# Router on the unnormalised rows, output projection by column halves, softmax per block, expert choice per sequence

## The chip, the cores and the metric

The kernel runs on one core of a Trainium2 chip. The metric is the device time of one execution in microseconds; lower is better. A core has five engines that run side by side, each with its own queue: TensorE (PE) for matrix products, VectorE (DVE), ScalarE (ACT), GpSimd (POOL) and SyncE (SP), which here only issues transfers. They wait for one another on semaphores. SBUF is the on-chip memory with 128 partitions; PSUM takes TensorE's results.

## The reference

One hybrid encoder layer on two sequences of 512 tokens of 1024 channels, in float32. What matters here is its end:

```
mixed = concat(attn_out, lru_out)                  # (512, 1024) per sequence
x2    = x + mixed @ w_out
h2    = x2 * rsqrt(mean(x2^2) + eps) * norm2_g
aff   = softmax(h2 @ router_w)                     # 16 experts
gate_vals, tok_idx = top_k(aff.T, 64)              # each expert takes 64 of 512 tokens
xs    = h2[tok_idx]
ys    = (silu(xs @ w_gate[e]) * (xs @ w_up[e])) @ w_down[e] * gate_vals
y     = x2 + scatter_add(ys, tok_idx)
```

The choice is made per sequence; both sequences' 64 tokens form one tile of 128 rows for each expert.

## The kernel before

All products are split: an operand is written as a high part (fp32r) and the remainder, and `product` (L869) issues three matmuls, hi x hi, hi x lo, lo x hi. The 1024 tokens of both sequences are NB = 8 blocks of 128 rows; blocks 0 to 3 (BPS = 4) are sequence 0, blocks 4 to 7 are sequence 1. Before the part that changes come the input projection, the recurrent part and the attention.

**Output projection.** For each block b (L997) TensorE runs `project_out(b, k)` over KC = 8 slices k, each with six matmuls of 512 columns, three for each half of the 1024 columns, into two PSUM banks. For block 0 the slices 0 to 5 are done inside the attention's last slots. In the same loop, one block later, come eight transposes of h2 (L933, for block b-1), and two blocks later the router's products (L1013, 8 slices, 16 matmul instructions, for block b-2). The last rounds of the loop have no projection left. SP loads the residual x_again (one buffer) once x2 of the block before is done (L456), stores x2 into y and h2 into the DRAM tensor h2_rows.

**VectorE** adds x_again for the whole block (L1305), waits for ScalarE's sum of squares (L777) and root (L779), computes the reciprocal and a Newton step (L1311, L1109 to L1112), and writes h2 = x2 * rstd * gain (L1315). ScalarE also copies the transposed h2 out of PSUM (L786).

**Softmax and expert choice.** After the logits of all eight blocks VectorE takes the maximum, ScalarE the exponential (L789), VectorE the sum, the reciprocal and the product (L1321 to L1329). TensorE transposes the affinities, so that experts lie on partitions: 0 to 15 for sequence 0 and 32 to 47 for sequence 1, 512 columns each (L1025). Then CAP // 8 = 8 rounds over 48 partitions (L1336): max gives the eight largest, max_index their positions, match_replace strikes them out. The lists are stacked and transposed (L1343 to L1349); `routed` tells GpSimd that the indices are there.

**Into the experts.** When the output projection is over, SP issues five weight loads (1 MB each) of expert 0, then the last stores, then, once these have landed, one more for up and two for down (L480, L482), then the gate weights of expert 1 (L490; the last two of them after both first gathers have landed). GpSimd computes the low parts of the first six gate rows (L574), copies an index column, and gathers 128 rows of h2 (L586). TensorE transposes them, ScalarE and VectorE write xsT_hi and xsT_lo (L807, L1360), and the first product waits for both halves of xsT_lo. From there on the expert loop runs, 24 rows of weights an expert, each row six matmuls.

Nothing is planned by a tool: every engine's order is that of the written code, and the waits in it are on counts.

Of the kernel before, what the change touches and what calls it, by code (L numbers as in the profile page):

```python
# [38 lines left out]
def layer_program(nc, x0, x1, norm1_g, w_in, q_norm_g, k_norm_g, conv_w, conv_b, lru_w_r, lru_b_r,  # L39
# [44 lines left out]
    vec_rows = at("vec_rows", 1536, [44, P], F32)  # L84
    vecs = at("vecs", 2048, [P, 44], F32)
# [7 lines left out]
    V_CONVW, V_CONVB, V_BR, V_BI, V_LAM = 0, 16, 20, 28, 36  # L93
# [64 lines left out]
    h2T = at("h2T", QUIET, [P, 2, KC, P], F32)  # L158
# [4 lines left out]
    aff_pad = at("aff_pad", R5 + 512, [P, BPS, 48], F32)  # L163
    aff_stat = at("aff_stat", R5 + 512 + 768, [P, 3, NB], F32)
# [11 lines left out]
    aff_work = at("aff_work", R1, [48, 2, S], F32)  # L176
    top_val = at("top_val", R1 + 4 * K, [48, CAP], F32)
    top_idx = at("top_idx", R1 + 4 * K + 256, [48, CAP], U32)
    stacked = at("stacked", R1 + 4 * K + 512, [E, 2, P], F32)
# [21 lines left out]
    assert RAW0 >= R1 + 128 * K  # L201
# [43 lines left out]
    h2T_done, h2T_out, logits_done = sem("h2T_done"), sem("h2T_out"), sem("logits_done")  # L245
    aff_shifted, aff_exp_done, aff_done, affT_done = sem("aff_shifted"), sem("aff_exp_done"), sem("aff_done"), sem("affT_done")
    stacked_done, stackedT_done, routed = sem("stacked_done"), sem("stackedT_done"), sem("routed")
    pad_zeroed = sem("pad_zeroed")
# [136 lines left out]

    block = ctx.enter_context(nc.Block())

    @block.sync
    def _(sp):
        rows = [(0, conv_w[0].rearrange("t (c p) -> (t c) p", p=P)), (16, conv_b[0].rearrange("(c p) -> c p", p=P)),  # L390
                (20, lru_b_r[0].rearrange("d (c p) -> (d c) p", p=P)), (28, lru_b_i[0].rearrange("d (c p) -> (d c) p", p=P)),
                (36, lru_lambda[0].rearrange("d (c p) -> (d c) p", p=P))]
# [60 lines left out]
        for b in range(NB):  # L453
            if b:
                sp.wait_ge(x2_done, b)
# [9 lines left out]
        sp.wait_ge(outproj_done, NB)  # L465
# [4 lines left out]
        sp.wait_ge(x2_done, NB)  # L470
# [8 lines left out]
        sp.wait_ge(h2T_done, 2 * NB)  # L479
# [25 lines left out]
    def _(pool):  # L505
# [62 lines left out]
        pool.wait_ge(scores_done, UNITS)  # L568
        pool.memset(aff_pad[:, :, :], 0.0).then_inc(pad_zeroed, 1)

        pool.wait_ge(outproj_done, NB)
# [3 lines left out]
        pool.wait_ge(routed, 2)  # L575
# [3 lines left out]
        for e in range(4):  # L579
            p = e % 2  # L580
            if e >= 2:
                pool.wait_ge(xsT_done, 2 * (e - 1))
            pool.tensor_copy(idx_now[:, p:p + 1], idx_all[:, e:e + 1]).then_inc(idx_copied, 1)
            pool.wait_ge(idx_copied, e + 1)
            pool.sem_inc(gather_ready, 1)
            pool.indirect_dma_start(xs[:, p, :], None, h2_rows, bass.IndirectOffsetOnAxis(ap=idx_now[:, p:p + 1], axis=0)).then_inc(xs_loaded[p], 16)  # L586
# [12 lines left out]
        with pool.Fori(0, (E - 4) // 2) as pair:  # L599
            e = pair * 2  # L600
            for parity in range(2):
                pool.wait_ge(xsT_done, e * 2 + (2 * parity + 6))
                pool.tensor_copy(idx_now[:, parity:parity + 1], idx_all[:, bass.ds(e + (parity + 4), 1)]).then_inc(idx_copied, 1)  # L603
                pool.wait_ge(idx_copied, e * 2 + (5 + 2 * parity))
# [3 lines left out]
                scatter_step(e + parity, e * 2 + (6 + 2 * parity))  # L608
        for e in range(E - 4, E):
            scatter_step(e, 4 + 2 * (E - 4) + e - (E - 4) + 1)  # L610

    @block.scalar
    def _(act):
# [155 lines left out]
        for b in range(NB + 1):  # L769
            if b < NB:  # L770
                act.wait_ge(x2_done, b + 1)
                if b:
                    act.wait_ge(h2_done, b)
                if b >= 2:
                    act.wait_ge(h2_stored[b % 2], 16 * (b // 2))
                    act.wait_ge(h2T_done, 2 * (b - 1))
                act.activation(h2[:, b % 2, :], x2[:, b % 2, :], ACT.Square, accum_out=sumsq1[:, b:b + 1]).then_inc(sumsq2_done, 1)  # L777
                act.wait_ge(sumsq2_done, b + 1)
                act.activation(root1[:, b:b + 1], sumsq1[:, b:b + 1], ACT.Sqrt, scale=1.0 / D, bias=eps).then_inc(root2_done, 1)  # L779
            if b:  # L780
                c = b - 1
                for h in range(2):
                    act.wait_ge(h2T_done, 2 * c + h + 1)
                    if c >= 2:
                        act.wait_ge(logits_done, c - 1)
                    act.activation(h2T[:, c % 2, 4 * h:4 * h + 4, :], bank[:, 4 + h, :].rearrange("p (k t) -> p k t", k=4),  # L786
                                   ACT.Copy).then_inc(h2T_out, 1)
        act.wait_ge(aff_shifted, 1)
        act.activation(aff_e[:, :, :], aff_e[:, :, :], ACT.Exp).then_inc(aff_exp_done, 1)  # L789
# [43 lines left out]
        act.wait_ge(outproj_done, NB)  # L833
        for j in range(SPLIT):
            hi_row(0, 0, raw_gate, gate_loaded, 16, j)
        turn_hi(xsT_hi[:, 0, :, :], xsT_done, 0, xsT_hi_done)
# [31 lines left out]
    def _(pe):  # L868
# [7 lines left out]
        for step in steps:  # L876
# [13 lines left out]
            elif kind == "vectors":  # L890
                pe.wait_ge(vec_loaded, 5 * 16)
                pe.transpose(bank[:, 0, 0:44], vec_rows[:, :], ident[0:44, 0:44]).then_inc(vec_t, 1)
# [43 lines left out]
        def project_out(b, k):  # L936
# [9 lines left out]
            for h in range(2):  # L946
# [50 lines left out]
        for b in range(NB + 2):  # L997
            if b < NB:
                if b >= 2:
                    pe.wait_ge(x2_done, b - 1)  # L1000
                if b == 1:
                    pe.wait_ge(probT_lo_done, UNITS)
                    pe.wait_ge(mixA_lo_done, HEADS // 2)
                for k in range(0 if b else WO_EARLY, KC):
                    ins = project_out(b, k)
                ins.then_inc(outproj_done, 1)
            c = b - 2
            if 0 <= c < NB:
                pe.wait_ge(h2T_out, 2 * (c + 1))
                if c == 0:  # L1010
                    pe.wait_ge(consts3_loaded, 2 * 16)
                for k in range(KC):
                    ins = pe.matmul(bank[:, 7, c * E:(c + 1) * E], h2T[:, c % 2, k, :], router[:, k, :], start=(k == 0), stop=(k == KC - 1))  # L1013
                ins.then_inc(logits_done, 1)
            c = b - 1
            if 0 <= c < NB:
                pe.wait_ge(h2_done, c + 1)
                for h in range(2):
                    if c:
                        pe.wait_ge(h2T_out, 2 * (c - 1) + h + 1)  # L1020
                    transposes(4 + h, [h2[:, c % 2, (4 * h + i) * P:(4 * h + i + 1) * P] for i in range(4)], h2T_done)

        pe.wait_ge(aff_done, 1)
        for b in range(BPS):
            ins = pe.transpose(bank[0:48, 6, b * P:(b + 1) * P], aff_pad[:, b, :], ident[:, :])  # L1025
        ins.then_inc(affT_done, 1)
        pe.wait_ge(stacked_done, 1)
        for i in range(2):
            ins = pe.transpose(bank[:, 5, i * E:(i + 1) * E], stacked[:, i, :], ident[0:E, 0:E])
        ins.then_inc(stackedT_done, 1)  # L1030


        def rows(first, m, first_bank, l_hi, l_lo, between, inc_last=1):

            for j in range(8):
                if j in between:
                    between[j]()
                pe.wait_ge(row_lo, first + (8 * m + j + 1))
# [21 lines left out]
        pe.wait_ge(xsT_lo_done, 2)  # L1060
# [379 lines left out]
```

## Time and profile before

| | us |
|---|---|
| median of three runs | 1089.27 (1089.07 to 1091.78) |
| span of the profiled execution, first to last instruction | 1093.4 |
| output projection, from block 0's last slices | 377.3 to 470.7 |
| from there to the first expert product | 470.7 to 516.1 |
| experts | 516.1 to 1093.4 |

The profiled execution's own time is given as its span; a clocked time without the profiler is not on record for it, and the span is 4.1 us above the median of the timed runs. Over the whole span PE is busy 91%, DVE 75%, ACT 65%, POOL 31%. "Busy" is time in instructions; an engine that waits for a semaphore is idle. In a timeline row the bracket holds the idle time ahead of the instruction and what ended it; "x8" merges eight instructions that follow one another.

### The profile page before, as it was taken

How to read it: one execution, taken by the hardware profiler on the slowest of the kernel's cores; microseconds unless marked ns; L12 is line 12 of the kernel's file. 1: busy time of each engine (PE TensorE's matmuls, PEld its weight loads, DVE VectorE, ACT ScalarE, POOL GpSimd, SP SyncE). 2: the span in 40 equal slices, each digit the busy share in tenths (PEclk: the TensorE clock that was granted, in tenths of full speed). 3: DMA queues.
4: the chain of work that ended last, by engine and by line, in shares of the span. 5: the costliest groups of instructions: out<-in, count | busy, mean ns of one | idle time of the engine just before them, and what ended most of it. 6: DMA issues, size and time to landing. Idle time of an engine off the chain costs nothing.

```text
span 1093.4 us, 14829 instructions
## 1 busy us (share of the span) xinstructions
PE 997.1 (91%) x4935; PEld 828.8 (76%) x4935; DVE 818.3 (75%) x1012; ACT 714.0 (65%) x949; POOL 341.5 (31%) x192
## 2 busy tenths in 40 slices
PE   3999999848899999962999999999999999999994
PEld 3789998737776788851788888888888888888883
DVE  5658767977788432235798889888988889888973
ACT  6357777257889321130787779777887779877872
POOL 0000002653356000024043465335643465323220
PEclk9999999968999999965999999999999999999998
DMA  7111110000210463366799999999999999999942
GB/s 252 42 44 44 44 52 1 1 1 1 74 44 1 157 247 119 115 250 249 255 365 385 392 390 404 379 389 389 402 384 383 392 384 402 388 375 386 336 157 37
DMA packets 75233, 248.96 MB, mean 228 GB/s; under 512 B 9356, under 2 KB 16568, under 8 KB 75192
## 3 DMA queue, kind: packets, MB, share of 16 engines
q1 hardware_dynamic: 70584, 231.64, 55.3%
q0 software_dynamic: 4608, 16.78, 6.1%
q8 instruction: 25, 0.41, 0.2%
q14 instruction: 16, 0.13, 0.0%
HBM read 231.63 MB, written 16.78 MB: 227 GB/s over the span
## 4 chain that ended last, share of the span: by engine, by line
PE 75%; DVE 11%; ACT 7%; issue 4%; DMA 1%; SPq 0%; ACTq 0%; POOL 0%; DVEq 0%; POOLq 0%
PE bank L871 23%; PE bank L873 22%; PE bank L872 22%; PE bank L933 5%; DVE e_lo L1355 2%; ACT e_hi L802 2%; PE bank L1013 1%; DVE swapped L1139 1%; PE bank L976 1%; ACT prob L762 1%; PE bank L977 1%; DMA x_nat<-in_x_prompt_dram 1%; DVE k_pair L1157 1%; DVE q_pair L1155 1%; DVE row_stat L1281 1%
## 5 line engine op out<-in xcount | busy, mean ns | idle before, releaser
L871 PE MATMUL bank<-e_hi,xsT_hi 128*128 128x512 f32 x512 | 202.2, 395 | 1.6 <-DVE xsT_lo L1360 1.4
L872 PE MATMUL bank<-e_lo,xsT_hi 128*128 128x512 f32 x512 | 200.3, 391 | 0.0
L873 PE MATMUL bank<-e_hi,xsT_lo 128*128 128x512 f32 x512 | 200.2, 391 | 0.0
L590 POOL COPY idx_now<-idx_all 128x1 uint32 (+1 forms) x16 | 157.0, 9811 | 26.7 <-DMA y_dram<-ys,idx_now 26.6
L802 ACT ACTIVATE e_hi<-raw_gate 128x1024 fp32r<-128x1024 f32 x128 | 134.7, 1061 | 36.2 <-PE bank L873 34.6
L1355 DVE TENSOR_TENSOR e_lo<-raw_down,e_hi 128x1024 fp32r<-128x1024 f32 x128 | 146.9, 1221 | 2.4 <-ACT e_hi L802 1.2
L1355 DVE TENSOR_TENSOR e_lo<-raw_up,e_hi 128x1024 fp32r<-128x1024 f32 x128 | 146.8, 1220 | 1.4 <-ACT e_hi L802 1.3
L1355 DVE TENSOR_TENSOR e_lo<-raw_gate,e_hi 128x1024 fp32r<-128x1024 f32 x122 | 141.2, 1220 | 5.6 <-ACT e_hi L802 5.6
L802 ACT ACTIVATE e_hi<-raw_up 128x1024 fp32r<-128x1024 f32 x128 | 126.5, 1056 | 1.7 <-PE bank L873 0.3
L802 ACT ACTIVATE e_hi<-raw_down 128x1024 fp32r<-128x1024 f32 x128 | 125.0, 1059 | 0.4 <-PE bank L873 0.3
L871 PEld LDWEIGHTS bank<-e_hi,xsT_hi 128*128 128x128 f32 x512 | 96.8, 189 | 22.4 <-DVE xsT_lo L1360 1.8
L873 PEld LDWEIGHTS bank<-e_hi,xsT_lo 128*128 128x128 f32 x512 | 96.7, 189 | 20.3
L872 PEld LDWEIGHTS bank<-e_lo,xsT_hi 128*128 128x128 f32 x512 | 96.9, 189 | 19.6
L871 PE MATMUL bank<-e_hi,hidT_hi 128*128 128x512 f32 x256 | 103.1, 403 | 4.9 <-DVE e_lo L1355 3.3
L873 PE MATMUL bank<-e_hi,hidT_lo 128*128 128x512 f32 x256 | 100.1, 391 | 0.0
L872 PE MATMUL bank<-e_lo,hidT_hi 128*128 128x512 f32 x256 | 99.8, 390 | 0.0
L603 POOL COPY idx_now<-idx_all 128x1 uint32 x12 | 13.4, 1116 | 213.1 <-PE bank L933 213.1
L594 POOL DMA_INDIRECT y_dram<-ys,idx_now x16 | 44.5, 2782 | 79.3 <-ACT ys L817 54.4
L564 POOL TENSOR_SCALAR prob<-prob,row_stat 128x512 f32<-128x512 f32 x64 | 46.8, 731 | 69.9 <-DVE row_stat L1290 69.9
L807 ACT ACTIVATE hidT_hi<-bank 128x512 fp32r<-128x512 f32 x32 | 17.4, 595 | 78.5 <-PE bank L933 78.5
L871 PEld LDWEIGHTS bank<-e_hi,hidT_hi 128*128 128x128 f32 x256 | 48.0, 188 | 20.6 <-DVE e_lo L1355 8.9
L1360 DVE TENSOR_TENSOR hidT_lo<-bank,hidT_hi 128x512 fp32r<-128x512 f32 x32 | 20.6, 686 | 51.1 <-ACT hidT_hi L807 51.1
(210 smaller groups left out, 2143.6 us busy)
## 6 DMA issues: line engine op xcount, KB each, us to landing
raw_gate<-in_exp_w_gate_dram SPq DMA_DIRECT2D x64, 1024.0 KB, 10.3
raw_up<-in_exp_w_up_dram SPq DMA_DIRECT2D x64, 1024.0 KB, 8.1
raw_down<-in_exp_w_down_dram SPq DMA_DIRECT2D x64, 1024.0 KB, 6.9
w_raw<-in_w_in_dram SPq DMA_DIRECT2D x7, 1024.0 KB, 5.4
wo_raw<-in_w_out_dram SPq DMA_DIRECT2D x8, 512.0 KB, 4.2
y_dram<-x SPq DMA_DIRECT2D x8, 512.0 KB, 5.1
h_rows<-h SPq DMA_DIRECT2D x8, 512.0 KB, 3.4
x_nat<-in_x_prompt_dram SPq DMA_DIRECT2D x4, 512.0 KB, 5.6
```

The costliest lines, as they stand in the source:

```text
L564: pool.tensor_scalar(prob[:, u % PROB_SLOTS, :], prob[:, u % PROB_SLOTS, :], row_stat[:, 2, u:u + 1], 1.0, ALU.mult, ALU.mult).then_inc(pr ...
L590: pool.tensor_copy(idx_now[:, 2:3], idx_all[:, bass.ds(e, 1)] if not isinstance(e, int) else idx_all[:, e:e + 1]).then_inc(idx_copied, 1)
L594: pool.indirect_dma_start(y, bass.IndirectOffsetOnAxis(ap=idx_now[:, 2:3], axis=0), ys[:, :], None, compute_op=ALU.add).then_inc(scattered ...
L603: pool.tensor_copy(idx_now[:, parity:parity + 1], idx_all[:, bass.ds(e + (parity + 4), 1)]).then_inc(idx_copied, 1)
L802: act.activation(e_hi[:, (8 * m + j) % SPLIT, :], raw[:, j // 2, j % 2, :], ACT.Copy).then_inc(row_hi, inc)
L807: act.activation(out[:, 4 * h:4 * h + 4, :], bank[:, 6 + h, :].rearrange("p (k t) -> p k t", k=4), ACT.Copy).then_inc(out_done, 1)
L871: pe.matmul(out, l_hi, r_hi, start=first, stop=False)
L872: pe.matmul(out, l_hi, r_lo, start=False, stop=False)
L873: return pe.matmul(out, l_lo, r_hi, start=False, stop=last)
L933: ins = pe.transpose(bank[:, out_bank, i * P:(i + 1) * P], piece, ident[:, :])
L1355: dve.tensor_tensor(e_lo[:, slot, :], raw[:, j // 2, j % 2, :], e_hi[:, slot, :].bitcast(F32), ALU.subtract).then_inc(row_lo, inc)
L1360: dve.tensor_tensor(out[:, 4 * h:4 * h + 4, :], bank[:, 6 + h, :].rearrange("p (k t) -> p k t", k=4), hi[:, 4 * h:4 * h + 4, :].bitcast(F3 ...
```

## The change

The router takes x2 and not h2. The gain norm2_g is multiplied into the router's weights once, on GpSimd (it comes as eight more rows of `vec_rows`), and 1/rms of a row is applied in the softmax: the exponential has it as its scale. So x2 is transposed (x2T), not h2. h2 is still computed and stored for the gathers.

The projection of a block runs by column halves: all eight slices for columns 0 to 511, then all for 512 to 1023, each with its own count in outproj_done (now 2 per block). x2, the squares, the transposes, the copies and h2 are done by halves. Transposes and router products of the block before stand inside the block's projection.

The softmax is done for each block by itself, and each block's affinities are transposed by themselves, one block later. The expert choice of sequence 0 runs on VectorE in the iterations of blocks 4, 5 and 6 (three, three, two rounds); that of sequence 1 after the last block. The rounds write into four groups of 16 partitions (0, 32, 64, 96), so that one max_index finds the positions of four rounds (two finds per sequence, not eight). ScalarE and VectorE copy the lists into `stacked`. In ScalarE's last block two copies of lists (`stack_vals`) stand ahead of the exponential, and two among the first gate rows.

GpSimd's gathers for experts 0 to 3 read idx_all directly, without a copy; the first product waits for one half of xsT_lo, the other half is waited for at slice 4.

The diff, cut to what carries it (layouts, semaphores and renamed counts left out):

```diff
@@ scalar: one half of a block; the root; the softmax of a block @@
+        def half_stat(b, h):
+            act.wait_ge(x2_done, 2 * b + h + 1)
...
+            act.activation(h2[:, b % 2, cols], x2[:, b % 2, cols], ACT.Square, accum_out=x2_stat[:, h, b:b + 1]).then_inc(sumsq2_done, 1)
+            act.wait_ge(x2T_done, 2 * b + h + 1)
...
+            act.activation(x2T[:, b % 2, 4 * h:4 * h + 4, :], bank[:, 4 + h, :].rearrange("p (k t) -> p k t", k=4),
+                           ACT.Copy).then_inc(x2T_out, 1)
+        def root(b):
+            act.wait_ge(root_bias_done, b + 1)
...
+            act.activation(small[:, 122:123], eps, ACT.Exp)
+        def soft_exp(b):
+            act.wait_ge(aff_shifted, b + 1)
...
+            act.activation(aff_e[:, b, :], bank[:, 7, b * E:(b + 1) * E], ACT.Exp, scale=rstd1[:, b:b + 1], bias=aff_stat[:, 1, b:b + 1],
+                           accum_out=aff_stat[:, 2, b:b + 1]).then_inc(aff_exp_done, 1)
+            if b < NB - 1:
+                act.activation(small[:, 122:123], eps, ACT.Sqrt)
...
+        for b in range(NB):
+            half_stat(b, 0)
             if b:
+                soft_exp(b - 1)
+            if b == BPS + 2:
+                stack_vals(0, 0)
+            half_stat(b, 1)
+            root(b)
+            if b == BPS + 3:
+                stack_vals(0, 1)
+        soft_exp(NB - 1)
@@ tensor @@
+        def turn_x2(b, h):
+            pe.wait_ge(x2_done, 2 * b + h + 1)
...
+        def turn_aff(b):
+            pe.wait_ge(aff_done, b + 1)
...
+        for b in range(NB):
...
+            ks = list(range(0 if b else WO_EARLY, KC))
+            middle = len(ks) // 2
+            for h in range(2):
                 if b >= 2:
+                    pe.wait_ge(x2_done, 2 * (b - 2) + h + 1)
+                for k in ks[:middle]:
+                    project_out(b, k, (h,))
+                if h == 0 and b:
+                    turn_x2(b - 1, 1)
+                if h == 1:
+                    turn_x2(b, 0)
+                    if b:
+                        turn_aff(b - 1)
+                for k in ks[middle:]:
+                    ins = project_out(b, k, (h,))
                 ins.then_inc(outproj_done, 1)
+                if h == 0 and b:
+                    logits_of(b - 1, 0)
+                    logits_of(b - 1, 1)
+        logits_of(NB - 1, 0)
+        turn_x2(NB - 1, 1)
+        logits_of(NB - 1, 1)
+        turn_aff(NB - 1)
@@ vector @@
+        def top_round(s, r):
...
+            dve.max(top_val[rows, eight], work[rows, f, :]).then_inc(top_done, 1)
...
+                link(dve.match_replace(work[rows_next, f_next, :], top_val[rows, eight], work[rows, f, :], -1.0))
+            if r % QUADS == QUADS - 1:
...
+                dve.max_index(top_idx[0:used, eight], top_val[0:used, eight], work[0:used, f, :]).then_inc(found, 1)
...
+        for b in range(NB):
+            x2_half(b, 0)
+            root_bias(b)
+            if b:
+                soft_shift(b - 1)
+                soft_share(b - 1)
+            x2_half(b, 1)
+            rstd2(b)
+            if b == NB - 1:
+                soft_shift(b)
+            h2_half(b, 0)
+            if b == NB - 1:
+                soft_share(b)
+            h2_half(b, 1)
+            if b == BPS:
+                affinities(0, BPS)
+            if b >= BPS and b < NB - 1:
+                for r in range(3 * (b - BPS), min(3 * (b - BPS) + 3, CAP // 8)):
+                    top_round(0, r)
+            if b == NB - 1:
+                affinities(BPS, NB - 1)
+        affinities(NB - 1, NB)
         for r in range(CAP // 8):
+            top_round(1, r)
```

## Rows read from the trace of the kernel before

**Rows 1.** Busy time by stage: bounds, length, then busy us and instructions of each engine.

```profile
377.30:470.70 93.40, 93.37 (x479) 79.56 (x479) 25.42 (x59) 17.37 (x35) 0.00 (x0) 1.00 0.47 164
...
470.70:516.10 45.40, 14.92 (x77) 13.12 (x76) 24.68 (x61) 12.08 (x17) 17.01 (x12) 0.54 0.74 277
...
516.10:1093.40 577.30, 559.29 (x2552) 458.67 (x2552) 489.12 (x456) 439.06 (x473) 228.63 (x59) 0.99 0.93 351
```

**Rows 2.** Timeline of TensorE between two blocks: start us, length, engine, line, operation.

```profile
402.85 1.85 PE L1013 MATMUL bank<-router,h2T 128*128 128x16 f32 x16
...
404.55 1.07 PE L933 MATMUL bank<-ident,h 128*128 128x128 f32 x8
...
405.38 0.48 PE L871 MATMUL bank<-wo_hi,mixA_hi 128*128 128x512 f32 x1
```

**Rows 3.** Timeline of VectorE over one block of the projection.

```profile
416.58 1.23 DVE L1305 TENSOR_TENSOR x<-bank,x_again 128x1024 f32<-128x1024 f32 x1 [8.43 <-PE bank L873]
...
419.42 0.16 DVE L1311 RECIPROCAL small<-small 128x1 f32<-128x1 f32 x1 [0.24 <-ACT small L779]
...
420.39 1.29 DVE L1315 SCALAR_TENSOR_TENSOR h<-x,small,g2b 128x1024 f32<-128x1024 f32 x1
...
430.10 1.23 DVE L1305 TENSOR_TENSOR x<-bank,x_again 128x1024 f32<-128x1024 f32 x1 [8.43 <-PE bank L873]
```

**Rows 4.** Timeline of ScalarE in a block, and its table load behind the last.

```profile
417.83 1.06 ACT L777 ACTIVATE h<-x 128x1024 f32<-128x1024 f32 x1 [11.08 <-DVE x L1305]
...
418.80 0.19 ACT L777 ACTIVATION_READ_ACCUMULATOR h<-x 128x1 f32 x1
...
419.22 1.07 ACT L786 ACTIVATE h2T<-bank 128x512 f32<-128x512 f32 x2
...
480.48 1.28 ACT L789 ACT_TABLE_LOAD   x1
```

**Rows 5.** Landing times of x_again's loads, then of the gathers into xs.

```profile
DMA to landing us min/median/max: 3.2/4.1/9.1
...
DMA to landing us min/median/max: 4.4/8.0/8.8
```

**Rows 6.** Timeline of VectorE in the expert choice and behind it.

```profile
487.92 0.69 DVE L1339 MAX8 top_val<-aff_work 48x8 f32<-48x512 f32 x1
...
488.64 0.08 DVE L1340 MATCH_VALUE_LOAD top_idx<-top_val,aff_work 48x8 f32 x1
...
489.42 0.08 DVE L1342 MATCH_VALUE_LOAD aff_work<-top_val,aff_work 48x8 f32 x1
...
505.46 0.18 DVE L1343 CAST stacked<-top_idx 16x64 f32<-16x64 uint32 x1
...
506.74 0.17 DVE L1348 CAST idx_all<-bank 128x16 uint32<-128x16 f32 x1 [0.49 <-PE bank L1029]
...
514.50 0.69 DVE L1360 TENSOR_TENSOR xsT_lo<-bank,xsT_hi 128x512 fp32r<-128x512 f32 x1 [7.51 <-ACT xsT_hi L807]
```

**Rows 7.** Timeline of GpSimd: the subtractions and the first gather.

```profile
486.20 13.91 POOL L574 TENSOR_TENSOR e_lo<-raw_gate,e_hi 128x1024 fp32r<-128x1024 f32 x6 [124.33 <-ACT e_hi L802]
...
508.18 1.18 POOL L586 DMA_INDIRECT xs<-h_rows,idx_now  x1 [0.93 <-POOL idx_now L583]
```

**Rows 8.** Timeline of SyncE: the first weight loads behind the last stores.

```profile
489.10 0.38 SPq L449 DMA_DIRECT2D raw_up<-in_exp_w_up_dram  x1
```

**Rows 9.** Timeline of TensorE: the first tokens, and the first expert product.

```profile
512.75 1.94 PE L933 MATMUL bank<-ident,xs 128*128 128x128 f32 x8 [6.05 <-DMA xs<-h_rows,idx_now]
...
516.11 0.79 PE L871 MATMUL bank<-e_hi,xsT_hi 128*128 128x512 f32 x1 [1.41 <-DVE xsT_lo L1360]
```

**Rows 10.** Busy time by stretch again; the figure after POOL is the granted clock.

```profile
215.00:218.00 3.00, 0.16 (x2) 0.00 (x0) 3.00 (x4) 1.49 (x5) 3.00 (x4) 1.00 0.00 0
...
218.00:225.00 7.00, 3.83 (x19) 3.86 (x19) 6.96 (x14) 4.38 (x9) 3.71 (x4) 0.51 0.01 2
...
516.00:522.00 6.00, 5.89 (x14) 4.64 (x15) 1.28 (x2) 1.35 (x2) 0.70 (x1) 0.51 0.72 265
```

More of the change, by code:

```diff
@@ L384, in v_in, with aff_bank, stack @@
         return qkv[:, :, QK:QKV].rearrange("p b (g w) -> p b g w", g=KVH)
+    def aff_bank(b):
+        return 4 if b == NB - 1 else 6
+    def stack(copy, s, find, what, top, done):
+        for q in range(QUADS):
+            slot = CAP * s + 32 * find + 8 * q
+            ins = copy(stacked[:, what, slot:slot + 8], top[32 * q:32 * q + E, 8 * find:8 * find + 8])
+        ins.then_inc(done, 1)
     block = ctx.enter_context(nc.Block())
@@ L768, in _ @@
                 split_wo_hi(k, half)
[L769 to L779, printed above, removed]
-            if b:
[L781 to L787, printed above, removed]
@@ new lines, in stack_vals @@
+        def stack_vals(s, find):
+            act.wait_ge(top_done, CAP // 8 * s + QUADS * (find + 1))
+            copy = lambda out, top: act.activation(out, top, ACT.Copy)
+            stack(copy, s, find, 1, top_val, vals_stacked)
+            if find == 0:
+                act.wait_ge(found, FINDS * s + 1)
+                stack(copy, s, find, 0, top_idx, idx_stacked)
+        act.activation(small[:, 122:123], eps, ACT.Sqrt)
+        for b in range(NB):
+            half_stat(b, 0)
+            if b:
+                soft_exp(b - 1)
[5 more added lines that the diff above has]
+                stack_vals(0, 1)
@@ L945, in project_out @@
             hi, lo, i = (mixA_hi, mixA_lo, k) if k < ATTN_W // P else (mixL_hi, mixL_lo, k - ATTN_W // P)
-            for h in range(2):
+            for h in halves:
                 cols = slice(h * 512, (h + 1) * 512)
@@ L1023, in _, with logits_of @@
[L1023 to L1027, printed above, removed]
+        def turn_x2(b, h):
+            pe.wait_ge(x2_done, 2 * b + h + 1)
+            if b:
+                pe.wait_ge(x2T_out, 2 * (b - 1) + h + 1)
+            transposes(4 + h, [x2[:, b % 2, (4 * h + i) * P:(4 * h + i + 1) * P] for i in range(4)], x2T_done)
+        def logits_of(b, h):
+            pe.wait_ge(x2T_out, 2 * b + h + 1)
+            if b == 0 and h == 0:
+                pe.wait_ge(router_done, 1)
+            if b and h == 0:
+                pe.wait_ge(aff_exp_done, b)
+            for k in range(4 * h, 4 * h + 4):
+                ins = pe.matmul(bank[:, 7, b * E:(b + 1) * E], x2T[:, b % 2, k, :], router[:, k, :], start=(k == 0), stop=(k == KC - 1))
+            if h:
+                ins.then_inc(logits_done, 1)
@@ L1037, in rows @@
                     between[j]()
+                if isinstance(first, int) and first == 0 and m == 0 and j == 4:
+                    pe.wait_ge(xsT_lo_done, 2)
                 pe.wait_ge(row_lo, first + (8 * m + j + 1))
@@ L1299, in _, with x2_half @@
                 split_wo_lo(k, half)
-        for b in range(NB):
-            dve.wait_ge(outproj_done, b + 1)
+        def x2_half(b, h):
+            dve.wait_ge(outproj_done, 2 * b + h + 1)
             dve.wait_ge(xa_loaded, 16 * (b + 1))
```

227 lines of the change are left out of this document (127 added, 100 removed).

## The prediction

> **What bounds the kernel now.** I cut the span into stages by each engine's busy time [rows 1]. In the output projection (377.3 to 470.7 us) TensorE is busy 93.37 of 93.40 us: it is the bound, and any wait put on it there is paid in full. From the last product (470.7) to the first expert product (516.1) TensorE works 14.9 of 45.4 us: a serial chain over PE, ACT, DVE and DMA. The expert stage is TensorE's again (559.3 of 577.3 us); the change leaves its loops alone but for index copies, so it only starts earlier or later. Two quantities decide: how much later the last output product ends, and how much shorter the chain behind it gets.
>
> TensorE's order in the projection: a block's 48 products, 16 router instructions in 1.70 us (402.85 to 404.55), 8 transposes in 0.83 [rows 2]. VectorE adds a block every 13.52 us (416.58, 430.10) [rows 3], so a product takes (13.52 - 1.70 - 0.83)/48 = 0.229 us: 2.72 for a group of 12, 10.9 for a block. Nothing waits.
>
> **The change: the projection.** I follow one new block b from its first product (t = 0).
>
> Work moved in. Before the last product there stood 6 groups of 8 transposes and 5 of router products; now 15 half groups, 7 router groups and 7 single transposes of affinities (0.13 each, from 1.07 for 8). That is 1.5 x 0.83 + 2 x 1.70 + 0.9 = 5.6 us later. The tail sum below is without them.
>
> Stalls, the term that I weigh most. PE's queue in the second half is: four k, turn_x2(b,0), turn_aff(b-1), four k. turn_aff(b-1) waits for soft_share(b-1) on DVE, that waits for soft_exp(b-1), and ACT's order puts soft_exp(b-1) behind the copy of x2T(b,0), which waits for turn_x2(b,0), the PE instruction just ahead. So PE idles through copy, exponential, accumulator read and two small DVE steps. A half copy is 0.53 to 0.6 (1.07 for two), the read 0.19 [rows 4]; I take 0.2 for a small activation and 0.195 for a DVE step with its semaphore, since five of them lie between 419.42 and 420.39 [rows 3]. 0.6 + 0.2 + 0.2 + 0.4 + drain 0.2 = 1.6 us, in blocks 1 to 7. Behind the waiting transpose stand twelve ready products; nobody else has work for PE. In block 1 x_again comes late, since four expert loads run beside it (its slowest landing was 9.1 us against 4.1 [rows 5]): 0.6 more.
>
> Blocks 5 to 7 have more: DVE runs search rounds there ahead of x2_half(b,0), on which turn_x2(b,0) waits. Its clock: root(b-1) sits on ACT behind the copy of x2T(b-1,1), whose transposes end at 3.4; root at 4.0, DVE's reciprocal and Newton to 5.35, two halves of h2 (1.29 whole [rows 3]) to 6.7. A search's max is 0.72 (487.92 to 488.64), a find 0.78 (to 489.42); from 487.92 to 505.46 there are eight of each and seven match-replaces, which leaves 0.79 for one of these [rows 6]. A round of max and replace is 1.5. Block 5: copy 0.7 and three rounds, 4.5: DVE is free at 11.9. x2_half takes 0.69 (as 514.50 [rows 6]), so turn_x2 starts at 12.65, not 10.3: 2.35 idle, then 1.8 behind it, since the root's bias and two softmax steps now come after it: 4.15. Block 6: three rounds and a find, 5.3: free at 12.0, 4.2 idle. Block 7: two rounds without the last replace, a find, four copies of the list: 3.85, free at 10.6, idle 2.75. Stalls: 2.2 + 3 x 1.6 + 4.15 + 4.2 + 2.75 = 18.1 us. Bounds: 7 x 1.2 = 8.4 if DVE's rounds fitted in and the small steps overlapped, 25 if each block lost 3.5.
>
> The last output product thus ends 23.7 us later. The two table loads per block (1.28 each [rows 4]) stand where ACT waits anyway, one after root (4.2 to 5.6), one after soft_exp (12 to 13.5); without that cover each would cost 1.28 in seven blocks. The half squares, the smaller maxima and POOL's scaling of the router (before block 1) cost PE nothing for the same reason.
>
> **The tail**, from the end of the last product. x2_half to 0.7; four transposes to 1.5; copy to 2.1; eight router instructions 0.85 (1.70/2) to 3.1, beside them root and Newton to 3.45. Shift to 3.9. ACT has to load the Exp table and then copy four value lists (4 x 0.2) before soft_exp: 4.55, done at 5.0. Share to 5.4, transposing to 5.8 beside the second half of h2, two copies to 6.85. Then eight rounds of the second sequence: before, 487.92 to 505.46 is 17.54 for eight with eight finds [rows 6]; six finds of 0.78 go: 12.85, to 19.7. Stacking and its transpose take about what they took (505.46 to 506.74 was 1.28): the index copy starts at 20.9, where before it was 506.74 - 470.7 = 36.0.
>
> The gather. Before it began at 508.18 [rows 7], 1.44 after the index copy started. The POOL copy (0.19) and its semaphore go, the issue stays: I take 0.9 (bounds 0.2 and 1.4). It needs the last h2 and x2 rows in DRAM; SP saw them land at 489.10 [rows 8], 18.4 after the last product, and will at about 18.5 again, since five weight loads stand ahead of the stores. So the gather at 21.8 is not held by them. But SP issues the next weights at 18.5: up, two down, two gate, 5 MB. At the 351 GB/s of the expert stage [rows 1] that is 15 us. Before, they were through at about 504, and the gather at 508.18 had the engines to itself and landed in 4.4; under load the median is 8.0 and the slowest 8.8 [rows 5]. Now it falls into them: I take 8.0, and keep 4.4 for the range. Landed at 29.8.
>
> From the first token transpose (512.75, 0.13 behind the landing) to the first product (516.11) it was 3.36 us, 1.94 of it transposes at 1.2 GHz [rows 9]. Waiting for one half of xsT_lo instead of two takes off the second half's share, one copy and one subtract behind each other's first: some 0.9. First product at 29.8 + 0.1 + 3.4 - 0.9 = 32.4, before 45.4: 13.0 gained; 16.6 with an undisturbed gather.
>
> POOL's six subtractions (13.91 us together [rows 7]) end at about 20.3, as ACT stops for the lists after the fourth row; just under the gather. Expert stage: same length. The start: one more small load ahead of the third x_nat, 0.3.
>
> **Sum**: 23.7 - 13.0 + 0.3 = +11.0 us. The span was 1093.4, 4.1 above the median of the runs; as a difference it gives 1089.3 + 11.0 = 1100.3 us.
>
> **TensorE's clock.** At 215 to 218 PE did 0.16 us of work at a granted clock of 1.00, and in 218 to 225 it had 0.51, its 1.2 GHz level; between 516 and 522 fourteen products ran at 0.51, 0.43 us apiece [rows 10]. So an idle PE was followed by the lower clock, and blocks 5 and 6 have 4.2 us of idleness each, broken only by four transposes. The Trainium skill (TensorE: Matmul & The Clock Gate, "HAM oscillation — how this bites in real kernels") says that a kernel whose matrix work is broken by waits starts each stretch at the lower clock. That speaks against this change. By it the sum would be rival A's; by the plain sum, 1100.3. I leave it out of the likeliest case, as the other five blocks lie idle for far less than that stretch did, and the two could escape.
>
> **Rivals.**
> A. The clock falls in blocks 5 and 6. The twelve products left in each cost 0.43 for 0.23, 2.4 us, more if the next block begins slow (218 to 225 was 7 us long, so up to 3.5): +5 to +7, 1105 to 1107.
> B. The gather lands in about 4.4 us although loads run: 1096.7. For: the first gather is small (0.5 MB). Against: the loaded median.
> C. Faster. The search instructions cost by rows, 16 now against 48: at a third, eight rounds lose 7.5 us and blocks 5 to 7 their 6.3 us of excess: 1086.5. It decides below about half of today's price. Against: on DVE 128 rows by 512 elements take 0.69 [rows 6], a max over 48 rows by 512 takes 0.69 too.
> D. The change doesn't stall PE as I say, because ACT's exponential is ready sooner: without the 1.6 us terms (11.2) the time is 1089, no change. Against: the order of three queues, which leaves no other way round.
>
> **Chances.** Forecast 0.42; A 0.23; B 0.15; C 0.10; D 0.10, of which 0.02 is faster, where B comes on top. A difference under 0.3%, 3.3 us, can't be told from none. Faster 0.12, same 0.08, slower 0.80. Range 1087 to 1107: down to C's and D's times, up to A's upper end.
>
> **What would show it.** In the new trace: PE idle about 1.6 us ahead of each affinity transpose, released by DVE's share; 2.4 ahead of the x2 transposes in blocks 5 and 6, released by x2; the last output product near 494; rounds of 1.50; the first gather landing after 8 us, first expert product near 527; expert stage 577 us. A last output product before 480 would overthrow the forecast, as would a first expert product before 516.

## The result and the profile after

The changed kernel takes 1110.41 us (median of 4 runs, 1108.58 to 1111.44), against 1090.35 for the kernel before (4 runs beside it): a ratio of 1.0177, interval 1.0154 to 1.0199, or 17 to 22 us slower. Its span is 1109.0 us. The way was forecast, the size was not: 11.0 us were expected, and the time lies above the range, which ended at 1107. One run of a later kernel and one of before beside it took over 4000 us; they are left out of the ranges given here.

The same three stages as in [rows 1], by busy time of the changed kernel (bounds, length, then PE, PEld, DVE, ACT, POOL, granted clock, DMA share, GB/s):

```profile
374.05:498.56 124.51, 109.14 (x530) 88.74 (x530) 47.08 (x142) 47.45 (x105) 0.00 (x0) 0.93 0.35 123
498.56:531.40 32.84, 5.58 (x31) 4.41 (x31) 18.89 (x48) 13.55 (x32) 16.21 (x8) 0.54 0.90 349
531.40:1109.00 577.60, 559.61 (x2552) 459.24 (x2552) 489.93 (x457) 439.05 (x474) 224.33 (x58) 0.99 0.94 353
```

Counted from the first product behind the wait for wo_lo of slice 6 (377.33 before, 374.06 now), the projection took 93.3 us and takes 124.5: 31.2 more. The stage behind it took 45.4 and takes 32.8: 12.6 less. The expert stage is as it was, 577.6. That is +18.6, and 18.9 with the expert stage's own 0.3 (577.3 before); the medians differ by 20.1, and no stage of the two traces holds the rest. The 0.3 expected for the start can't be seen, since the projection's start varies by more than that between executions. The difference of the two spans is only 15.6, because before's projection began 3.3 us later in its trace, and most of that is the clock, in a part of the kernel that the change leaves alone. First before, then after (the figure after POOL is the granted clock):

```profile
44.10:47.40 3.30, 3.30 (x9) 2.52 (x9) 2.63 (x18) 2.53 (x3) 0.00 (x0) 0.50 0.01 2
245.40:252.20 6.80, 5.72 (x23) 4.65 (x22) 4.61 (x9) 3.69 (x9) 1.66 (x3) 0.50 0.00 0
```

```profile
44.10:47.40 3.30, 3.30 (x16) 2.73 (x15) 2.72 (x18) 2.40 (x3) 0.00 (x0) 1.00 0.01 2
245.40:252.20 6.80, 5.26 (x35) 4.34 (x34) 5.43 (x13) 5.33 (x13) 2.77 (x4) 1.00 0.00 0
453.40:460.20 6.80, 5.40 (x14) 4.24 (x15) 0.75 (x5) 2.36 (x5) 0.00 (x0) 0.50 0.00 0
473.90:480.70 6.80, 5.67 (x14) 4.47 (x15) 0.65 (x4) 3.64 (x13) 0.00 (x0) 0.50 0.00 1
494.40:497.80 3.40, 3.40 (x10) 2.62 (x9) 0.00 (x0) 0.52 (x2) 0.00 (x0) 0.50 0.00 0
```

At 44 us there are nine matmuls instead of sixteen in 3.3 us, and the same instructions start 1.7 us later in before's trace behind it than in the other. At 245 us before's clock is still low and the changed kernel's is up again, and another 1.3 us come on top. Both kernels' runs spread over 3 us.

The last three of these stretches lie in the projection, in blocks 5, 6 and 7. Together they are 17 us at the lower clock, in which one product starts 0.43 us behind the other (455.83 to 456.26 us) and not 0.23 (461.10 to 461.33). Who made PE wait there (total us, times, longest):

```profile
PE bank L1075 <- DVE aff L1428: 10.6, 7, 1.5
...
PE bank L987 <- DVE x L1389: 4.5, 3, 2.0
```

Block 5 on TensorE. Columns: start, length, engine and instruction; a number in brackets is the idle time ahead of it and what ended it. Two such gaps lie close together, and a product behind them (L925 to L927) is listed with 0.63 us, and from 460.2 on with 0.40:

```profile
452.63 0.66 PE L987 MATMUL bank<-ident,x 128*128 128x128 f32 x4 [1.93 <-DVE x L1389]
454.80 0.38 PE L1075 MATMUL bank<-ident,aff 128*16 128x128 f32 x1 [1.52 <-DVE aff L1428]
...
455.83 0.63 PE L927 MATMUL bank<-wo_hi,mixL_lo 128*128 128x512 f32 x1
...
460.63 0.40 PE L927 MATMUL bank<-wo_hi,mixA_lo 128*128 128x512 f32 x1
```

The chain that ends the second gap, on ScalarE and then on VectorE (copy of x2T, exponential, its accumulator, reciprocal, share), and the search instructions: the instruction behind a max (here the replace, in [rows 6] the find) starts 0.72 later, on 16 rows as on 48, and a find over 112 rows takes 0.69:

```profile
453.32 0.60 ACT L801 ACTIVATE x2T<-bank 128x512 f32<-128x512 f32 x1
453.82 0.36 ACT L815 ACTIVATE aff_e<-bank,aff_stat,small 128x16 f32<-128x16 f32 x1
454.09 0.19 ACT L815 ACTIVATION_READ_ACCUMULATOR aff_e<-bank,aff_stat,small 128x1 f32 x1
```

```profile
447.31 0.68 DVE L1454 MAX8 top_val<-work 16x8 f32<-16x512 f32 x1
448.03 0.08 DVE L1458 MATCH_VALUE_LOAD work<-top_val,work 16x8 f32 x1
...
454.31 0.16 DVE L1427 RECIPROCAL aff_stat<-aff_stat 128x1 f32<-128x1 f32 x1 [0.52 <-ACT aff_e L815]
454.51 0.23 DVE L1428 TENSOR_SCALAR aff<-aff_e,aff_stat 128x16 f32<-128x16 f32 x1
...
468.49 0.69 DVE L1461 FIND_INDEX8 top_idx<-top_val,work 112x8 uint32<-112x512 f32 x1
```

The tail: lists transposed, tokens, first expert product, first gather issued, and the landing times of the first four gathers ([rows 5, 7, 9]):

```profile
519.79 0.36 PE L1108 MATMUL bank<-ident,stacked 16*128 16x16 f32 x2 [15.33 <-DVE stacked L401]
528.90 1.94 PE L987 MATMUL bank<-ident,xs 128*128 128x128 f32 x8 [8.75 <-DMA xs<-h_rows,idx_all]
531.40 0.79 PE L925 MATMUL bank<-e_hi,xsT_hi 128*128 128x512 f32 x1 [0.56 <-DVE xsT_lo L1505]
```

```profile
521.26 1.17 POOL L606 DMA_INDIRECT xs<-h_rows,idx_all  x1 [2.16 <-DVE gate_all L1494]
```

```profile
DMA to landing us min/median/max: 4.5/7.8/8.8
```

### The profile page after: what moved, and what is told of

Its sections match the earlier page's. It is cut to its first block, busy times and chain, and to the rows that moved or that the text cites. A ratio compares the mean times of both kernels' runs of the same rounds, so it can differ in the third digit from the quotient of the medians.

```text
span 1109.0 us, 15087 instructions
## 1 busy us (share of the span) xinstructions
PE 1000.9 (90%) x4939; PEld 827.8 (75%) x4939; DVE 833.9 (75%) x1084; ACT 745.4 (67%) x1034; POOL 338.3 (31%) x190
## 4 chain that ended last, share of the span: by engine, by line
PE 46%; DVE 4%; ACT 2%; issue 2%; DMA 1%; ACTq 0%; POOL 0%; DVEq 0%; POOLq 0%
PE bank L925 15%; PE bank L927 15%; PE bank L926 15%; PE bank L987 2%; DVE e_lo L1500 2%; ACT e_hi L853 2%; DMA xs<-h_rows,idx_all 1%; DVE top_val L1454 1%; DVE work L1458 1%; ACT hidT_hi L858 0%; DVE top_idx L1461 0%; DVE h L1413 0%; ACTq L852 0%; POOL y_dram L614 0%; DVE x L1389 0%
## 5 line engine op out<-in xcount | busy, mean ns | idle before, releaser
L925 PE MATMUL bank<-e_hi,xsT_hi 128*128 128x512 f32 x512 | 201.7, 394 | 0.8 <-DVE xsT_lo L1505 0.6
L927 PE MATMUL bank<-e_hi,xsT_lo 128*128 128x512 f32 x512 | 199.9, 390 | 0.0
L925 PEld LDWEIGHTS bank<-e_hi,xsT_hi 128*128 128x128 f32 x512 | 96.7, 189 | 21.5 <-DVE e_lo L1500 1.0
L927 PEld LDWEIGHTS bank<-e_hi,xsT_lo 128*128 128x128 f32 x512 | 96.6, 189 | 20.2
L925 PE MATMUL bank<-e_hi,hidT_hi 128*128 128x512 f32 x256 | 103.3, 404 | 4.8 <-DVE e_lo L1500 3.3
L927 PE MATMUL bank<-e_hi,hidT_lo 128*128 128x512 f32 x256 | 100.8, 394 | 0.0
L623 POOL COPY idx_now<-idx_all 128x1 uint32 x12 | 13.7, 1144 | 212.7 <-PE bank L987 212.7
L614 POOL DMA_INDIRECT y_dram<-ys,idx_now x16 | 39.6, 2477 | 85.2 <-ACT ys L868 54.1
L925 PEld LDWEIGHTS bank<-e_hi,hidT_hi 128*128 128x128 f32 x256 | 48.5, 189 | 20.6 <-DVE e_lo L1500 8.9
```

The costliest lines, as they stand in the source:

```text
L614: pool.indirect_dma_start(y, bass.IndirectOffsetOnAxis(ap=idx_now[:, 2:3], axis=0), ys[:, :], None, compute_op=ALU.add).then_inc(scattered ...
L925: pe.matmul(out, l_hi, r_hi, start=first, stop=False)
L927: return pe.matmul(out, l_lo, r_hi, start=False, stop=last)
```

## Experiments

"After" is the changed kernel; "last product" is the last one of the output projection, and all stage times are from the profiled execution of the kernel named. Before was timed again beside each group of runs: 1090.35 us beside after, 1092.41 beside the first four experiments, 1090.11 beside the last four. A difference between kernels of different groups is thus uncertain by some 2 us. Taken by the ratios to the before of the same group instead, the first four experiments are 7, 15, 11 and 20 us below after.

### Keeping the clock up: spare products in PE's gaps

```diff
+        def fill(b, n):
+            for i in range(n):
+                pe.matmul(bank[:, 2 * ((b + 1) % 2) + 1, :], mixA_hi[:, i % 4, 0:P], wo_hi[i % 4][:, 0:512], start=True, stop=True)
...
                 if h == 1:
+                    if b in (5, 6):
+                        fill(b, 9)
                     turn_x2(b, 0)
+                    if b in (5, 6, 7):
+                        fill(b, 6)
                     if b:
                         turn_aff(b - 1)
```

> The changed kernel with 9 spare products ahead of turn_x2(b,0) in blocks 5 and 6 and 6 spare products ahead of turn_aff(b-1) in blocks 5 to 7, written into a PSUM bank that is overwritten later; every wait stays. Clock theory: the fillers lie inside the 2.0 and 1.5 us in which PE waits anyway, the granted clock stays 1.00 in the projection, and the 12 + 12 + 8 products that ran at half the clock gain 0.2 us each: 6.5 us less than the changed kernel, 1104. Rival (the clock falls for another reason, or its loss is hidden by a later wait): the same time or up to 1 us more, 1110 to 1111.

Measured: 1103.68 us (1103.3 to 1106.91), 6.7 less than after. TensorE in block 5, and the projection as a whole:

```profile
450.49 2.20 PE L1080 MATMUL bank<-wo_hi,mixA_hi 128*128 128x512 f32 x9
452.57 0.66 PE L987 MATMUL bank<-ident,x 128*128 128x128 f32 x4
452.98 1.63 PE L1080 MATMUL bank<-wo_hi,mixA_hi 128*128 128x512 f32 x6
454.74 0.28 PE L1075 MATMUL bank<-ident,aff 128*16 128x128 f32 x1
...
455.09 0.39 PE L926 MATMUL bank<-wo_lo,mixL_hi 128*128 128x512 f32 x1
```

```profile
373.98:491.72 117.74, 110.42 (x566) 90.30 (x566) 47.09 (x142) 47.50 (x105) 0.00 (x0) 1.00 0.37 130
```

PE did more work and the kernel got faster. No wait was taken away: the affinity transpose of block 5 starts at 454.74, as it did at 454.80. The products behind it take 0.39 us instead of 0.63, and the projection takes 117.7 us instead of 124.5 at a granted clock of 1.00. So 6.8 us were the clock, and the idle gaps brought it down: filled, they did not. The rival, by which the spare products would only have added work, fell.

### The affinity transpose at the end of the block

```diff
                 if h == 1:
                     turn_x2(b, 0)
-                    if b:
-                        turn_aff(b - 1)
...
                 ins.then_inc(outproj_done, 1)
...
+                if h == 1 and b:
+                    turn_aff(b - 1)
```

> The changed kernel with turn_aff(b-1) moved from behind turn_x2(b,0) to the end of block b's second half; nothing else. Theory of the 1.5 us waits: seven of them go, 10.5 us. Blocks 5 and 6 keep 2.0 us of idleness ahead of turn_x2(b,0) and have dense products right behind it, so the clock should stay at 1.00: another 5 to 6.5 us. 1093.5 to 1095; 1100 if the clock still falls. Rival (the wait only moves, to the start of the next block or to DVE's rounds): 1108 to 1111.

Measured: 1097.8 us (7 runs, 1094.22 to 1098.84), 12.6 less than after; the kernel before had 1092.41 beside it. The projection, and two stretches in it:

```profile
376.94:486.29 109.35, 104.52 (x529) 85.90 (x529) 47.07 (x142) 47.45 (x105) 0.00 (x0) 0.97 0.39 140
450.00:453.30 3.30, 3.30 (x9) 2.56 (x8) 0.58 (x4) 2.19 (x5) 0.00 (x0) 0.50 0.00 0
467.10:470.30 3.20, 3.20 (x10) 2.54 (x9) 0.79 (x5) 2.96 (x9) 0.00 (x0) 0.50 0.01 3
```

109.4 us instead of 124.5, 15.1 less; the medians show 12.6, and this execution's projection began 2.9 us later than after's (376.94 against 374.06). No wait for an affinity is left, and the rival fell. The clock still fell twice, behind these waits for x2 in blocks 5 and 6, though for 3.4 us each and not 6.8:

```profile
449.05 0.66 PE L987 MATMUL bank<-ident,x 128*128 128x128 f32 x4 [1.93 <-DVE x L1389]
...
466.68 0.86 PE L987 MATMUL bank<-ident,x 128*128 128x128 f32 x4 [2.00 <-DVE x L1389]
```

So the time lies between the two figures expected, and what I had written as "should stay at 1.00" did not hold: one gap of 2 us in a block, with four transposes behind it and then products, was enough.

### The search rounds where VectorE idles

```diff
+        ahead = {5: (0, 1), 6: (3, 4), 7: (7,)}
+        behind = {5: (2,), 6: (5, 6)}
...
                 soft_share(b - 1)
+            for r in ahead.get(b, ()):
+                top_round(0, r)
             x2_half(b, 1)
+            for r in behind.get(b, ()):
+                top_round(0, r)
             rstd2(b)
...
-            if b >= BPS and b < NB - 1:
-                for r in range(3 * (b - BPS), min(3 * (b - BPS) + 3, CAP // 8)):
-                    top_round(0, r)
```

> The changed kernel with the search rounds of the first sequence moved on VectorE from behind h2_half(b,1) to places where VectorE idles: two behind soft_share and one behind x2_half(b,1) in block 5, two and two in block 6, the last behind soft_share of block 7. Same rounds, same finds. Theory: PE's waits for x2 of blocks 5 to 7 go (2.0 + 2.0 + 0.55 us) with the 0.3 each behind them, and with 1.5 us of idleness left per block the clock holds: 5.4 + 6.5 = about 12 less, 1098. Rival (VectorE is full there, so the wait moves to x2 of the second half and to the tail): 1107 to 1110.

Measured: 1099.71 us (1099.0 to 1102.35), 10.7 less than after. The projection, and PE's waits for affinities in it:

```profile
374.70:487.22 112.52, 101.68 (x530) 84.08 (x530) 46.78 (x142) 47.43 (x105) 0.00 (x0) 1.00 0.38 136
```

```profile
PE bank L1075 <- DVE aff L1428: 10.5, 7, 1.5
```

112.5 us, 12.0 less, at a clock of 1.00: the waits for x2 are gone, seven of 1.5 us are left and do not bring the clock down in this execution. The rival fell.

### Both moves

The last two edits together.

> Both moves together. Theory: no wait on PE in the projection, which ends about 23 us sooner than in the changed kernel: 10.5 of affinity waits, 5 of x2 waits, 6.5 of clock. 1087 to 1089, which is before's time or 1 to 3 us under it: the 12.6 us won in the tail less some 8 of PE work moved into the projection, less 2 of block 0 and of switching. Rival (the waits cover each other, so that removing both gives no more than one): about 1094 to 1098.

Measured: 1090.49 us (10 runs, 1089.41 to 1093.49) against 1092.41 for before; ratio 0.9991, interval 0.9978 to 1.0005, no difference. The projection and the stage behind it (PE waits for x2 once in the projection, 0.3 us):

```profile
373.67:475.27 101.60, 100.96 (x529) 83.72 (x529) 45.94 (x138) 47.45 (x105) 0.00 (x0) 1.00 0.43 151
475.27:509.71 34.44, 5.31 (x32) 4.13 (x31) 19.73 (x53) 13.54 (x32) 16.07 (x8) 0.57 0.92 354
```

101.6 us, 22.9 less than after, as expected. Against before it is 8.3 more: PE is busy for 7.6 us more (101.0 against the 93.3 of a stage in which it never idled) and idles for 0.6; what the tail gains (34.4 against 45.4) is 11.0. Of the 12.6 won in the tail, 1.6 went. The first gather is issued 23.6 us behind the last product instead of 22.7, with round 7 and its list ahead of the last x2, and its tokens are there after 8.2 us instead of 7.5, beside the same weight loads.

### The gather ahead of the weights

The kernel with both moves, and on SP:

```diff
         sp.wait_ge(x2T_done, 2 * NB)
+        for p in range(2):
+            sp.wait_ge(xs_loaded[p], 16)
         load(raw_up, 0, w_up, 0, up_loaded)
```

> The kernel with both moves (turn_aff late, rounds in VectorE's idle places), and SP holds the 5 MB of weight loads behind the last stores until both first gathers have landed. Theory (the gather shares the DMA engines with them): the first gather lands 4.5 us after its issue instead of about 7.5, the first expert product is 3 us nearer to the last projection product (31.4 instead of 34.4), and the expert stage, whose weights come 5 to 8 us later than they could, does not notice: 3 less than without the hold, 1087.5. Rival (the held weights are late for the first expert): 1090 or more, with PE waits on rows 530 to 560.

Measured: 1086.23 us (10 runs, 1083.41 to 1088.4) against 1090.11 for before; ratio 0.9958, interval 0.9941 to 0.9974. First tokens, then the last two stages:

```profile
506.97 1.94 PE L989 MATMUL bank<-ident,xs 128*128 128x128 f32 x8 [5.71 <-DMA xs<-h_rows,idx_all]
```

```profile
478.72:509.47 30.75, 5.32 (x32) 4.14 (x31) 19.76 (x53) 13.55 (x32) 16.19 (x8) 0.59 0.65 240
509.47:1086.50 577.03, 559.03 (x2552) 458.49 (x2552) 489.81 (x457) 438.99 (x474) 224.05 (x58) 0.99 0.95 360
```

The gather was issued at 502.38, so its tokens were there after 4.5 us; with both moves alone it was 8.2 (498.89 to 507.1). The tail shrinks from 34.4 to 30.8, and the expert stage (577.0) does not miss the weights. The rival fell. The medians of the two kernels, of different groups, are 4.3 us apart, and by the ratios 3.6, which is about what the tail lost.

### Spare products while PE waits for the gather

The kernel with both moves, and on TensorE:

```diff
+        pe.wait_ge(row_lo, SPLIT)
+        for i in range(18):
+            pe.matmul(bank[:, 4, :], e_hi[:, i % SPLIT, 0:P], e_hi[:, i % SPLIT, 0:512], start=True, stop=True)
         pe.wait_ge(routed, 2)
         turn_tokens(16, 0)
```

> The kernel with both moves, and 18 spare products on PE while it waits for the first gather (a PSUM bank not in use yet). Clock theory: PE works at half clock until about 4 us into the expert stage, because it lay idle; with the spare products the granted clock is 1.00 at the first token transposes or soon behind them: 0.9 us of transposes and nine products' 1.8, 2.5 us less, 1088. Rival (the clock comes back no sooner, or the fillers delay the transposes): 1090.5 or more.

Measured: 1090.02 us (10 runs, 1088.35 to 1092.31), against 1090.49 without the products (by the ratios to before, 1.0001 against 0.9991): nothing. The reason is in the trace:

```profile
498.15 6.01 PE L1140 MATMUL bank<-e_hi 128*128 128x512 f32 x18
507.98 1.51 PE L987 MATMUL bank<-ident,xs 128*128 128x128 f32 x8 [3.82 <-DMA xs<-h_rows,idx_all]
```

```profile
501.70:508.30 6.60, 2.78 (x14) 2.04 (x13) 0.00 (x0) 0.00 (x0) 0.08 (x1) 1.00 1.02 410
508.50:515.20 6.70, 6.14 (x18) 4.68 (x16) 2.35 (x3) 2.25 (x3) 0.94 (x1) 0.50 0.89 342
```

The spare products did bring the clock to 1.00 at 501.6, and as they then ran twice as fast they were over at 504.2. PE idled for 3.8 us, and the clock was down again from 508.4 to 515.2, over the first expert products. The rival held, and for a reason I had not thought of: spare products counted at the lower clock end too early.

### All of it

Both moves, the hold, 12 spare products, soft_exp(7) ahead of the copies of lists, and the rounds at other places:

```diff
+        ahead = {5: (0, 1), 6: (4, 5)}
+        behind = {5: (2, 3), 6: (6, 7)}
...
-            if b == BPS + 3:
-                stack_vals(0, 1)
         soft_exp(NB - 1)
+        stack_vals(0, 1)
```

> Both moves; the gathers ahead of the held weights; 12 spare products while PE waits for the gather; the first sequence's last rounds and lists all behind x2_half of block 6, so that none stands ahead of the last x2; and the last exponential ahead of the lists' copies on ScalarE. Theory: 3 from the gather, 2.5 from the clock, 0.8 and 0.3 from the tail's queues, together 6.6 less than the kernel with both moves: 1084. Rival (these cover one another): 1087.

Measured: 1083.51 us (1081.18 to 1084.54); ratio to before 0.9929, interval 0.9905 to 0.9953, faster than both kernels. The first two stages, and the clock over the first expert products:

```profile
373.93:474.99 101.06, 100.72 (x529) 83.80 (x529) 46.68 (x142) 47.43 (x105) 0.00 (x0) 1.00 0.44 151
474.99:503.96 28.97, 9.28 (x45) 7.14 (x44) 19.25 (x49) 13.58 (x32) 16.33 (x9) 0.65 0.70 254
504.20:507.50 3.30, 3.30 (x9) 2.52 (x9) 0.30 (x1) 0.65 (x1) 0.51 (x1) 0.50 0.63 194
```

The tail is 29.0 us. It was 34.4 with both moves alone, so 5.5 us came out of it: 3.7 between the gather's issue and its tokens (4.6 us to the first transposes instead of 8.3), 1.3 ahead of the issue (22.3 instead of 23.6 us behind the last product) with the new orders on VectorE and ScalarE, and 0.45 between the first token transposes and the first product, from the clock. The clock gave less than the 2.5 us expected. The twelve spare products ended at 501.3, 0.6 us before the tokens; the transposes ran at full clock, and it fell again at 504.1 for the first products. The median met the 1084 expected, though not by the terms that it was added up from. The rival, 1087, fell.

### The small steps alone, on the kernel before

The kernel before, with direct gathers, the wait for one half of xsT_lo, and 12 spare products:

```diff
-            pool.tensor_copy(idx_now[:, p:p + 1], idx_all[:, e:e + 1]).then_inc(idx_copied, 1)
-            pool.wait_ge(idx_copied, e + 1)
...
+                if isinstance(first, int) and first == 0 and m == 0 and j == 4:
+                    pe.wait_ge(xsT_lo_done, 2)
...
+        for i in range(12):
+            pe.matmul(bank[:, 4, :], e_hi[:, i % SPLIT, 0:P], e_hi[:, i % SPLIT, 0:512], start=True, stop=True)
...
-        pe.wait_ge(xsT_lo_done, 2)
+        pe.wait_ge(xsT_lo_done, 1)
```

> The kernel before with only the small steps behind the expert choice: the first gathers read idx_all directly, the first product waits for one half of xsT_lo, and 12 spare products run on PE while it waits for the gather. No change to projection, softmax or search. Theory: 0.5 + 0.9 + 2.5, so 4 less than before, 1088. Rival (only the clock or only the waits count): 1 to 2.5 less.

Measured: 1088.14 us (10 runs, 1085.27 to 1091.61) against 1090.11; ratio 0.9980, interval 0.9961 to 0.9999. The stage behind the last product:

```profile
468.99:512.76 43.77, 19.51 (x91) 16.27 (x90) 24.05 (x61) 11.97 (x17) 16.36 (x9) 0.57 0.76 288
```

43.8 us instead of 45.4. The 2.0 us saved are half of what was expected and lie in the rival's 1 to 2.5; the interval, 0.1 to 4.3, excludes neither. The trace shows both effects, though. The issue of the gather came 0.3 us sooner behind the last product, the first token transposes and the copies behind them took 2.0 us instead of 3.4, and the spare products, which ended 0.3 us before the tokens, held the clock over the first expert products:

```profile
512.80:518.80 6.00, 6.00 (x27) 4.97 (x28) 2.95 (x3) 2.12 (x2) 0.71 (x1) 1.00 0.72 262
```

From the first expert product to the second expert's token transposes it was 8.3 us (512.76 to 521.05) instead of 11.0 (516.11 to 527.11). Yet the expert stage as a whole took 577.0 us against before's 577.3. In the last expert PE waits twice, for the hidden layer and, behind eight transposes of it, for its low part. In this execution the clock fell behind these waits; in before's, with the same two waits, it did not. This run, then before:

```profile
1061.55 1.09 PE L931 MATMUL bank<-ident,hid 128*128 128x128 f32 x8 [1.32 <-DVE hid L1370]
1064.21 0.80 PE L869 MATMUL bank<-e_hi,hidT_hi 128*128 128x512 f32 x1 [1.57 <-DVE hidT_lo L1363]
```

```profile
1063.40:1070.10 6.70, 5.89 (x14) 4.64 (x15) 6.52 (x7) 5.07 (x6) 0.18 (x1) 0.50 0.01 2
```

```profile
1066.00:1073.00 7.00, 4.11 (x21) 3.03 (x20) 4.82 (x6) 4.37 (x6) 0.19 (x1) 1.00 0.36 66
```

All ten traces have this pair of waits, 1.32 and 1.57 us. Behind it the clock stayed at 1.00 in four (before and the runs with the late affinity transpose, the hold, and the eighteen spare products), fell for 3.4 us in five and for 6.8 in this one. So the same gaps cost from nothing to about 2.5 us (an estimate: some twelve products at 0.43 us instead of 0.23), and single executions of two kernels can't be set against each other to less than that. What decides it no run here shows. The profiled execution took 1091.61 us, the longest of its ten.

## Why the prediction was wrong, step by step

**The bound.** Right: in the projection PE was the bound, each wait on it was paid, and in the tail the chain decided.

**The affinity wait.** Right. Seven waits of 1.50 to 1.52 us released by VectorE's share, where 1.6 were forecast. Moving the instruction took them away. Rival D is refuted: the order of the three queues left no other way.

**The search rounds.** Right in place, a little too large: 1.93, 2.00 and 0.55 us of wait for x2 in blocks 5, 6 and 7, where I had 2.35, about 2.4 and 1.0. Rival C is refuted: the instruction behind a max starts 0.72 later with 16 rows as with 48. The waits of both kinds sum to 15.1 us in the profile; I had 18.1. In block 1 x_again was late for VectorE (by 2.8 us, at 387.66) but not for PE, so the 0.6 put down for it did not come.

**The work moved in.** 5.6 us forecast. With no waits and the clock up, the projection has 101.6 us against before's 93.3: 8.3. Two terms are missing. The run of products in a block is now broken by short fp32 matmuls in three places (in four with both moves), where before it was broken in one, and behind each the first product is 0.32 us ahead of the next and not 0.23 (390.85, 391.17, 391.39): by an estimate some 2 us in all. And in block 0 twelve products with four transposes among them and two short waits take 4.1 us (374.06 to 378.20) where twelve took 2.9 (377.33 to 380.18). By luck, what is too small here makes up for what was too large in the waits: 31.2 less the 6.8 of the clock leaves 24.4 us for work and waits, and 23.7 was forecast for them.

**The clock. This is the step that failed.** The prediction read the lower clock behind an idle PE from [rows 10], priced it in rival A at 5 to 7 us, and then left it out of the sum, "as the other five blocks lie idle for far less than that stretch did, and the two could escape". They did not escape: the clock fell in blocks 5 and 6 for 6.8 us each, and in block 7, which the prediction did not name, for 3.4. The term was put at nothing; the spare products measured it at 6.8 us of projection and 6.7 of time. Rival A had the mechanism and the size, with block 7 missing from it. The argument for an escape was drawn from blocks with one gap of 1.5 us each. With a gap of 2 us ahead of four transposes the clock fell each time that a trace has it unfilled, twice in the changed kernel and twice in the one with the affinity moved. An escape was not out of the question, though: the pair of 1.32 and 1.57 us in the last expert was passed at full clock in four traces of ten. The Trainium skill (TensorE: Matmul & The Clock Gate, "HAM oscillation — how this bites in real kernels") tells of a kernel in which each stretch behind a wait starts at the lower clock. Its waits are of 3 to 5 us, and blocks 5 to 7 showed the same with shorter ones; in blocks 1 to 4, with one gap of 1.5 us each, the granted clock stayed at 1.00.

**The tail.** Right: 32.4 us forecast, 32.8 measured, part by part. The gather's issue came 1.17 us behind the start of the index copy (0.9 forecast), and its tokens were there 7.5 us later, in the middle of the five loads issued from 517.17. Rival B is refuted for this kernel, and the hold showed why: without those loads it is 4.5. The DMA engines moved 411 to 420 GB/s from 521 to 529 us, where the prediction had reckoned with 351.

**The sum.** 31.2 - 12.6 = 18.6 by stages, inside the timed 17 to 22; the forecast had 23.7 - 13.0 + 0.3 = 11.0. Of the 7.6 between them 6.8 are the clock, 0.7 work and waits and 0.4 the tail, less the 0.3 of the start. The expert stage took 0.3 more. The medians differ by 20.1, another 1.2, and no trace shows where that lies. The range ended at 1107, which is 1100.3 and rival A's 7; before itself came out 1.1 us above the 1089.3 that the forecast started from, and so the clock's price alone filled the range and the rest fell outside.

## What to carry to other kernels

Before an instruction is put between the two halves of a bound engine's work, follow what it waits for through the other engines' orders: here the transpose of one block hung on a copy of the next block's, issued one instruction earlier, and moving it to the end of the block gave back all seven waits. When waits are added to a TensorE that was dense, price the clock with them in the likeliest case: in blocks 5 to 7 the gaps cost 9 us of waiting (1.93 + 2.00 + 0.55 + 3 x 1.5) and the slow products behind them 6.8 more. And when one profile is compared with another, look first where the clock of each was low. And work taken out of a serial tail is only won if the engine that bounds the stage before has room for it: 12.6 us came out of the tail here and 8.3 of work went into the projection even with every wait removed.

## What was not expected of the hardware

TensorE got faster by doing more: 36 spare products in gaps it could not use otherwise saved 6.7 us. Spare products before a wait did nothing where they ended 3.8 us before the tokens: they had lifted the clock at 501.6, and it was down again 4.2 us after the last of them. Where they ended 0.6 us before, the transposes had the full clock and the first products had not; where they ended 0.3 us before, both had it. And the clock differs between executions over the same work, in at least three places: a stretch of 3.4 us at 0.50 near 44 us is there in three of the ten traces; the stretch that begins near 230 us lasts 20.5 us in seven and 13.7 in three; and the pair of waits in the last expert, as told above. The three traces with the stretch at 44 us begin the output projection at 376.9 to 377.3 us, the others at 373.7 to 375.7.
